# Two weight tiles of a ring of four loaded by one transfer of 1 MB instead of two of 512 KB

## The chip, the cores and the metric

One of the eight cores of a Trainium2 chip runs the kernel. Its time is the device time of one execution in microseconds (us), 738.69 us as the median of three runs. The engines are TensorE (PE, matmuls, with its weight loads as PEld), VectorE (DVE), ScalarE (ACT), GpSimd (POOL) and SyncE (SP), which here only issues DMAs. Each runs its own list of instructions in order and waits on semaphores.

## The reference

A decoder block on x of 256 tokens by 2048, all in float32. After an RMS norm one wide projection gives, for 16 heads of width 128, q, k, v and a gate, then 8 forget logits and two merge gates of 2048. Two attention branches follow, each is projected back, and the two are merged, projected and normed:

```python
z = einsum('bsd,dn->bsn', h, w_in)                   # 2048 x (8 x 1024 + 8 + 2 x 2048)
oa = diff_attention(qa, ka, va, lam)                 # 8 heads, softmax of two maps, p0 - lam * p1
ya = (rmsnorm(oa, g_subln) * (1 - lam_init) * silu(ga)) @ w_proj_a
ob = forgetting_attention(qb, kb, vb, log_f)         # 8 heads, bias by the cumulative log forget gate
yb = (ob * silu(gb)) @ w_proj_b
m = sigmoid(ma) * ya + sigmoid(mb) * yb
y = rmsnorm(x + m @ w_out, g_final)
```

## The kernel before

**Work.** The weights stream from memory, most of them through a ring (165 MB in all pass SyncE's queue, since some tiles of the gates are loaded more than once), and each is used by TensorE with the 256 tokens as stationary operand. The unit is a *tile*: 128 rows (partitions) by 1024 columns, which holds two k-steps of 128 of a chunk of 512 output columns, 512 KB. A matmul runs at high precision as three products (`split_product`, lines 342 to 344): high part of the weights times high part of the tokens, high times low, low times high. So every weight tile goes through three stations:

1. SyncE loads it into `w_raw` (four slots, `RAW = 4`), or, for one kind of tile, into `chain`.
2. ScalarE writes the high part into `w_hi` (four slots, `RING = 4`), line 614; it first waits that TensorE has used the tile four before (`w_used`).
3. VectorE writes the low part, raw minus high, into `w_lo`, line 842. This frees the slot of `w_raw` (`lo_ready`).

**Jobs.** Tiles are numbered as jobs in the order in which TensorE uses them: head 0, forget logits and part of head 1, head 2 without mixing (`PLAIN_JOB` = 20), then from `MIXED_JOB` = 28 heads 3 to 15 with 8 tiles each, mixed one to one with tiles of the merge gates, then the projection of branch B (F), of branch A (D) and the output projection (O). A head tile has two k-steps for both halves of the tokens, 12 matmuls of 512 columns. H9.2 is tile 2 of head 9. F0 is chunk 0 of the projection of branch B, which is mixed with the last gates.

**The merge gates** are computed in four groups (one for each 512 columns), each by seven products (forms P1, P5, P6, P3, P7, P4, P2) of four tiles instead of eight, in the manner of Strassen: a tile of P5, P6, P7 and P4 is a difference of a loaded tile with the one kept in `chain`. VectorE makes it with `add` (lines 855 and 857; semaphore `added`), five jobs before TensorE needs it, in its list ahead of the low split of the tile before. In forms P5, P6 and P4 the sum stands in `chain`, so the raw slot is free when the add is done. P1 tiles are loaded into `chain` itself and are not in the ring. A gate tile has 6 matmuls.

**Ring numbers.** `RAW_NO` gives each ring tile its number r; its slot is r modulo 4. `load` (in SyncE's list) waits for the user of r - 4: `added` if it is a P5, P6 or P4 tile, `lo_ready` otherwise, and issues the load. Nothing else sets the order: all lists are written out ahead of time, with no scheduler. VectorE and ScalarE also do the softmax and the gates of one head per 16 jobs, between the splits.

Of the kernel before, what the change touches and what calls it, by code (L numbers as in the profile page):

```python
# [8 lines left out]
P = 128  # L9
# [12 lines left out]
CHUNK = 512  # L22
RING = 4
RAW = 4
TILES = 8
# [4 lines left out]
P1, P5, P6, P3, P7, P4, P2 = range(FORMS)  # L30
# [5 lines left out]
MERGE, PROJ, OUT = N_HEADS, N_HEADS + 8, N_HEADS + 12  # L36

FL_JOB, VG_JOB, PLAIN_JOB, MIXED_JOB = 8, 16, 20, 28
# [3 lines left out]
OUT_JOB = DIFF_JOB + 16  # L42
# [5 lines left out]
SUM_OF = {job: s for s, job in enumerate(SUM_JOB)}  # L48
# [33 lines left out]
HEAD_OF = {head_job(c, j): (c, j) for c in range(2, N_HEADS) for j in range(TILES)}  # L82
# [4 lines left out]
def sum_parts(s):  # L87
    return s // (FORMS * QUARTERS), s // QUARTERS % FORMS, s % QUARTERS
# [7 lines left out]
JOB_OF_RAW = {r: job for job, r in RAW_NO.items()}  # L96


def add_no(s):
    g, f, q = sum_parts(s)  # L100
    return 16 * g + {P5: 0, P6: 4, P7: 8, P4: 12}[f] + q + 1


def build(nc, x, xT, xg, consts_in, w_main, w_fl, g_final, out):
    fp32 = mybir.dt.float32
    fp32r = mybir.dt.float32r
    ALU = mybir.AluOpType
# [8 lines left out]
    with ctx:  # L116
# [139 lines left out]

        def wait_raw(engine, job):
            r = RAW_NO[job]
            engine.wait_ge(raw_loaded[r % RAW], 16 * (r // RAW + 1))

        def in_chain(job):
            return job in SUM_OF and sum_parts(SUM_OF[job])[1] in (P1, P5, P6, P4)
# [9 lines left out]
        @block.sync  # L272
        def _(sp):
            def source(job):

                if job < VG_JOB:
                    return w_main[job] if job < FL_JOB else w_fl[job - FL_JOB]
                if job < PLAIN_JOB:
                    return w_main[TILES + job - VG_JOB]
                if job in HEAD_OF:  # L280
                    c, j = HEAD_OF[job]
                    return w_main[8 * c + j - 4]
                if job in SUM_OF:
                    g, f, q = sum_parts(SUM_OF[job])
                    c, half = {P1: (MERGE, 0), P5: (MERGE + 4, 0), P6: (MERGE + 4, 1), P3: (MERGE + 4, 1), P7: (MERGE, 0),
                               P4: (MERGE, 1), P2: (MERGE, 1)}[f]
                    return w_main[8 * (c + g) + 4 * half + q - 4]
                if job in FOX_OF:
                    n, j = FOX_OF[job]
                    return w_main[8 * (PROJ + n) + j]  # L290
                if job in DIFF_OF:
                    n, j = DIFF_OF[job]
                    return w_main[8 * (PROJ + n) + j - 4]
                return w_main[8 * OUT + job - OUT_JOB - 4]

            def load(job):

                if job in SUM_OF:
                    g, f, q = sum_parts(SUM_OF[job])
                    if f == P1:  # L300
                        if g == 0:
                            sp.wait_ge(sums_ready, 4)
                        else:
                            sp.wait_ge(lo_ready, SUM_JOB[SUM_OF[job] - 2 * QUARTERS] + 1)
                        sp.dma_start(chain[:, q, :], source(job)).then_inc(chain_loaded[q], 16)
                        return
                r = RAW_NO[job]
                if r >= RAW:
                    user = JOB_OF_RAW[r - RAW]
                    if in_chain(user):  # L310
                        sp.wait_ge(added, add_no(SUM_OF[user]))
                    else:
                        sp.wait_ge(lo_ready, user + 1)
                sp.dma_start(raw_slot(job), source(job)).then_inc(raw_loaded[r % RAW], 16)

            for t in range(TILES):
                if t >= 4:
                    sp.dma_start(xT_sb[:, 2 * t:2 * t + 2, :], xT[:, 2 * t:2 * t + 2, :]).then_inc(x_loaded[t], 16)
                if t == 0:
                    sp.dma_start(w_raw[:, 0, 0:CHUNK], w_main[0][:, 0:CHUNK]).then_inc(first_half, 16)  # L320
                    sp.dma_start(w_raw[:, 0, CHUNK:2 * CHUNK], w_main[0][:, CHUNK:2 * CHUNK]).then_inc(raw_loaded[0], 16)
                else:
                    load(t)
            for job in range(TILES, OUT_JOB):
                load(job)

            sp.wait_ge(o_split, 4)
            sp.dma_start(x_res, x_v).then_inc(xres_loaded, 16)
            sp.wait_ge(og_ready, N_HEADS)
            sp.dma_start(g_rows, g_final.rearrange("(a n) -> a n", a=1).to_broadcast([P, D_MODEL])).then_inc(gf_loaded, 16)  # L330
            for job in range(OUT_JOB, JOBS):
                load(job)
            for m in range(M_TILES):
                for i, cols in enumerate((DVE_OUT, LAST_OUT)):
                    sp.wait_ge(out_ready[1], 2 * m + i + 1)
                    sp.dma_start(out_v[:, m, cols], yg[:, m, cols]).then_inc(out_stored, 16)
            sp.wait_ge(out_stored, 3 * M_TILES * 16)
# [966 lines left out]
```

## Time and profile before

| | |
|---|---|
| median of 3 runs | 738.69 us (738.66 to 739.47) |
| the profiled execution's own time | 738.65 us |
| its span in the profile | 736.8 us |
| TensorE, VectorE, ScalarE busy | 99%, 76%, 60% |
| loads of w_raw of 512 KB | 283, median 4.2 us from issue to landing |

Times are from the span's start. In a timeline a row is one instruction, or several equal ones in a row (xN): its start, its duration, engine, source line, operation, what it writes and reads. Consecutive instructions of an engine overlap a little, so the start of the next is earlier than start plus duration. `[0.65 <-DMA w_raw<-in_w_main]` says that the engine was idle for 0.65 us before it and that a load's landing ended this.

### The profile page before, as it was taken

The page shows a single profiled execution, that of the slowest core. Times are in us where ns is not written, and L with a number is a line of the kernel's source. Part 1 is how long each engine was busy: PE and PEld are TensorE (multiplying, and loading weights), DVE is VectorE, ACT ScalarE, POOL GpSimd, SP SyncE. Part 2 cuts the span into 40 slices and gives each one's busy share as a digit, 9 for nine tenths or more (in the row PEclk, how much of TensorE's full clock was granted, in tenths as well). Part 3 has the DMA queues.
Part 4 walks back from the last instruction along what each step waited for, and adds up shares of the span by engine and source line. Part 5 has one row for each costly group of instructions (what it writes and reads, how often), then busy time and mean ns, then how long its engine had stood idle before and what let it go on. Part 6 is the DMA issues. An engine that isn't in the chain of part 4 may idle for free.

```text
span 736.8 us, 9631 instructions
## 1 busy us (share of the span) xinstructions
PE 727.8 (99%) x3490; PEld 606.8 (82%) x3490; DVE 560.3 (76%) x723; ACT 438.7 (60%) x652; POOL 84.7 (12%) x105
## 2 busy tenths in 40 slices
PE   9999999999999999999999999999999999999995
PEld 6998888888888888888888888888888888888884
DVE  6785799788669778868878976898998657655552
ACT  7963767566656565665666666577667544444531
POOL 0000223103010201010302020202020000001110
PEclk9999999999999999999999999999999999999999
DMA  9778366777847676775576776576777656755542
GB/s 338 210 243 296 143 229 226 233 231 254 334 151 253 210 247 231 270 293 183 212 266 202 241 274 261 191 267 222 226 246 246 207 193 230 290 190 187 194 142 115
DMA packets 47230, 168.97 MB, mean 229 GB/s; under 512 B 5256, under 2 KB 5264, under 8 KB 46672
## 3 DMA queue, kind: packets, MB, share of 16 engines
q1 hardware_dynamic: 46064, 164.97, 64.8%
q10 hardware_dynamic: 864, 1.84, 0.7%
q0 software_dynamic: 256, 1.54, 0.6%
q8 instruction: 29, 0.48, 0.3%
q14 instruction: 17, 0.14, 0.1%
HBM read 166.23 MB, written 2.11 MB: 228 GB/s over the span
## 4 chain that ended last, share of the span: by engine, by line
PE 96%; issue 1%; DMA 1%; ACT 0%; DVE 0%; SPq 0%; DVEq 0%; POOLq 0%; POOL 0%
PE Z L342 29%; PE Z L344 29%; PE Z L343 29%; PE Z L503 3%; PE A L444 1%; PE A L410 1%; DMA w_raw<-in_w_main 1%; PE B L426 1%; PE Dk L435 1%; PE B L423 1%; PE C L453 0%; PE A L461 0%; PE B L461 0%; ACT w_hi L614 0%; PE A L515 0%
## 5 line engine op out<-in xcount | busy, mean ns | idle before, releaser
L842 DVE TENSOR_TENSOR w_lo<-w_raw,w_hi 128x1024 fp32r<-128x1024 f32 (+1 forms) x240 | 290.2, 1215 | 110.7 <-ACT w_hi L614 107.9
L614 ACT ACTIVATE w_hi<-w_raw 128x1024 fp32r<-128x1024 f32 (+1 forms) x235 | 243.6, 1044 | 184.3 <-PE Z L344 149.9
L342 PE MATMUL Z<-w_hi,hT_hi 128*128 128x512 f32 (+2 forms) x720 | 275.2, 382 | 0.1
L344 PE MATMUL Z<-w_hi,hT_lo 128*128 128x512 f32 (+2 forms) x720 | 273.6, 380 | 0.0
L343 PE MATMUL Z<-w_lo,hT_hi 128*128 128x512 f32 (+2 forms) x720 | 273.5, 380 | 0.0
L342 PEld LDWEIGHTS Z<-w_hi,hT_hi 128*128 128x128 f32 x720 | 135.3, 188 | 26.6 <-ACT w_hi L614 0.5
L344 PEld LDWEIGHTS Z<-w_hi,hT_lo 128*128 128x128 f32 x720 | 135.3, 188 | 25.6
L343 PEld LDWEIGHTS Z<-w_lo,hT_hi 128*128 128x128 f32 x720 | 135.3, 188 | 25.0
L342 PE MATMUL Z<-w_hi,sum_hi 128*128 128x512 f32 x256 | 101.2, 395 | 0.0
L344 PE MATMUL Z<-w_hi,sum_lo 128*128 128x512 f32 x256 | 99.8, 390 | 0.0
L343 PE MATMUL Z<-w_lo,sum_hi 128*128 128x512 f32 x256 | 99.7, 390 | 0.0
L614 ACT ACTIVATE w_hi<-x_and_g 128x1024 fp32r<-128x1024 f32 x64 | 67.8, 1059 | 51.1 <-DVE x_and_g L857 30.2
L842 DVE TENSOR_TENSOR w_lo<-x_and_g,w_hi 128x1024 fp32r<-128x1024 f32 x64 | 80.2, 1254 | 23.2 <-ACT w_hi L614 22.2
L857 DVE TENSOR_TENSOR x_and_g<-w_raw,x_and_g 128x1024 f32<-128x1024 f32 x48 | 59.2, 1233 | 4.9 <-DMA w_raw<-in_w_main 4.9
L344 PEld LDWEIGHTS Z<-w_hi,sum_lo 128*128 128x128 f32 x256 | 48.0, 188 | 10.1
L342 PEld LDWEIGHTS Z<-w_hi,sum_hi 128*128 128x128 f32 x256 | 48.1, 188 | 9.7 <-issue 0.3
L343 PEld LDWEIGHTS Z<-w_lo,sum_hi 128*128 128x128 f32 x256 | 48.1, 188 | 9.5
L1205 POOL TENSOR_TENSOR bias<-gates,c_nat 128x128 f32<-128x128 f32 (+1 forms) x16 | 16.3, 1037 | 151.6 <-DVE neg_max L978 144.3
L1235 POOL TENSOR_TENSOR o_rstd<-o_ms,neg_half 128x2 f32<-128x2 f32 x8 | 9.2, 1156 | 190.3 <-DVE o_ms L1055 190.3
L619 ACT ACTIVATE z_sb<-Z,rstd 128x512 f32<-128x512 f32 x29 | 18.4, 685 | 20.5 <-PE Z L344 19.6
L1223 POOL TENSOR_TENSOR rope_t<-z_sb,consts 128x64 f32<-128x64 f32 x32 | 17.2, 567 | 108.4 <-ACT z_sb L619 108.4
L855 DVE TENSOR_TENSOR w_raw<-x_and_g,w_raw 128x1024 f32<-128x1024 f32 x16 | 19.7, 1229 | 5.7 <-DMA w_raw<-in_w_main 5.7
(171 smaller groups left out, 545.5 us busy)
## 6 DMA issues: line engine op xcount, KB each, us to landing
w_raw<-in_w_main SPq DMA_DIRECT2D x283, 512.0 KB, 4.2
x_and_g<-in_w_main SPq DMA_DIRECT2D x16, 512.0 KB, 6.1
w_raw<-in_w_fl SPq DMA_DIRECT2D x8, 264.0 KB, 2.9
o_T<-in_x SPq DMA_DIRECT2D x1, 2048.0 KB, 8.0
x_and_g<-in_xT SPq DMA_DIRECT2D x4, 256.0 KB, 5.8
gates<-c_rows_dram POOLq DMA_DIRECT2D x1, 1024.0 KB, 7.8
z_sb<-in_g_final SPq DMA_DIRECT2D x1, 1024.0 KB, 10.0
x_and_g<-in_xT ACTq DMA_DIRECT2D x3, 256.0 KB, 7.9
```

The costliest lines, as they stand in the source:

```text
L342: pe.matmul(acc, a_hi, b_hi, start=first, stop=False)
L343: pe.matmul(acc, a_hi, b_lo, start=False, stop=False)
L344: return pe.matmul(acc, a_lo, b_hi, start=False, stop=last)
L503: mm = pe.matmul(Z[m][:], x_part[:, 2 * j + kk, m * P:(m + 1) * P], w_part[:, kk], start=(j == 0 and part == 0 and kk == 0), stop=(j == TI ...
L614: act.activation(w_hi[:, t % RING, 0:cols_of(t)], weights(t), ACT.Copy).then_inc(hi_ready, 1)
L619: act.activation(z_sb[:, c % Z_SLOTS, m], Z[(2 if c == 2 else 0) + m][:], ACT.Copy, scale=rstd[:, m:m + 1]).then_inc(evac[m], 1)
L842: dve.tensor_tensor(w_lo[:, t % RING, 0:n], weights(t), w_hi[:, t % RING, 0:n].bitcast(fp32), ALU.subtract).then_inc(lo_ready, 1)
L855: dve.tensor_tensor(raw, chain[:, q, :], raw, ALU.subtract).then_inc(added, 1)
L857: dve.tensor_tensor(chain[:, q, :], raw, chain[:, q, :], ALU.subtract).then_inc(added, 1)
L1205: pool.tensor_tensor(bias[:, sl].unsqueeze(1), rows.rearrange("p (h n) -> p h n", h=HEADS)[:, h:h + 1, 0:n], c_nat[:, m, h:h + 1].unsqueez ...
L1223: ins = pool.tensor_tensor(rope_t[:, i], u, v, ALU.mult)
L1235: pool.tensor_tensor(o_rstd[:], o_ms[:], neg_half[:], ALU.pow).then_inc(o_rstd_ready, 1)
```

## The change

From ring number 20 on (job 20, the first tile of head 2) two consecutive ring tiles r and r + 1, r even, are loaded by one DMA into two adjacent slots (0 and 1, or 2 and 3). The weights are laid out for this ahead of time in a second array, `w_pairs`, in which each partition's row holds both tiles, 8 KB; the 16 P1 tiles and the first 20 ring tiles are still read from `w_main`. The load waits for the users of r - 4 and of r - 3, both, and is issued at the place of r. Users of both tiles wait for the one semaphore of the even slot. The lists of TensorE, ScalarE, VectorE and GpSimd keep their instructions and their order.

```diff
--- before.py
+++ after.py
@@ -96,12 +96,43 @@
 JOB_OF_RAW = {r: job for job, r in RAW_NO.items()}
 
 
+def tile_index(job):
+
+    if job < FL_JOB:
+        return job
+    if job < PLAIN_JOB:
+        return TILES + job - VG_JOB
+    if job in HEAD_OF:
+        c, j = HEAD_OF[job]
+        return 8 * c + j - 4
+    if job in SUM_OF:
+        g, f, q = sum_parts(SUM_OF[job])
+        c, half = {P1: (MERGE, 0), P5: (MERGE + 4, 0), P6: (MERGE + 4, 1), P3: (MERGE + 4, 1), P7: (MERGE, 0),
+                   P4: (MERGE, 1), P2: (MERGE, 1)}[f]
+        return 8 * (c + g) + 4 * half + q - 4
+    if job in FOX_OF:
+        n, j = FOX_OF[job]
+        return 8 * (PROJ + n) + j
+    if job in DIFF_OF:
+        n, j = DIFF_OF[job]
+        return 8 * (PROJ + n) + j - 4
+    return 8 * OUT + job - OUT_JOB - 4
+
+
+FIRST_PAIR = RAW_NO[PLAIN_JOB]
+PAIRED = len(RAW_NO) - len(RAW_NO) % 2
+
+
+def in_pair(job):
+    return FIRST_PAIR <= RAW_NO[job] < PAIRED
+
+
 def add_no(s):
     g, f, q = sum_parts(s)
     return 16 * g + {P5: 0, P6: 4, P7: 8, P4: 12}[f] + q + 1
 
 
-def build(nc, x, xT, xg, consts_in, w_main, w_fl, g_final, out):
+def build(nc, x, xT, xg, consts_in, w_main, w_pairs, w_fl, g_final, out):
     fp32 = mybir.dt.float32
     fp32r = mybir.dt.float32r
     ALU = mybir.AluOpType
@@ -256,7 +287,7 @@
 
         def wait_raw(engine, job):
             r = RAW_NO[job]
-            engine.wait_ge(raw_loaded[r % RAW], 16 * (r // RAW + 1))
+            engine.wait_ge(raw_loaded[(r - r % 2 if in_pair(job) else r) % RAW], 16 * (r // RAW + 1))
 
         def in_chain(job):
             return job in SUM_OF and sum_parts(SUM_OF[job])[1] in (P1, P5, P6, P4)
@@ -273,25 +304,7 @@
         def _(sp):
             def source(job):
 
-                if job < VG_JOB:
-                    return w_main[job] if job < FL_JOB else w_fl[job - FL_JOB]
-                if job < PLAIN_JOB:
-                    return w_main[TILES + job - VG_JOB]
-                if job in HEAD_OF:
-                    c, j = HEAD_OF[job]
-                    return w_main[8 * c + j - 4]
-                if job in SUM_OF:
-                    g, f, q = sum_parts(SUM_OF[job])
-                    c, half = {P1: (MERGE, 0), P5: (MERGE + 4, 0), P6: (MERGE + 4, 1), P3: (MERGE + 4, 1), P7: (MERGE, 0),
-                               P4: (MERGE, 1), P2: (MERGE, 1)}[f]
-                    return w_main[8 * (c + g) + 4 * half + q - 4]
-                if job in FOX_OF:
-                    n, j = FOX_OF[job]
-                    return w_main[8 * (PROJ + n) + j]
-                if job in DIFF_OF:
-                    n, j = DIFF_OF[job]
-                    return w_main[8 * (PROJ + n) + j - 4]
-                return w_main[8 * OUT + job - OUT_JOB - 4]
+                return w_fl[job - FL_JOB] if FL_JOB <= job < VG_JOB else w_main[tile_index(job)]
 
             def load(job):
 
@@ -305,12 +318,19 @@
                         sp.dma_start(chain[:, q, :], source(job)).then_inc(chain_loaded[q], 16)
                         return
                 r = RAW_NO[job]
-                if r >= RAW:
-                    user = JOB_OF_RAW[r - RAW]
-                    if in_chain(user):
-                        sp.wait_ge(added, add_no(SUM_OF[user]))
-                    else:
-                        sp.wait_ge(lo_ready, user + 1)
+                if in_pair(job) and r % 2:
+                    return
+                for slot in (r, r + 1) if in_pair(job) else (r,):
+                    if slot >= RAW:
+                        user = JOB_OF_RAW[slot - RAW]
+                        if in_chain(user):
+                            sp.wait_ge(added, add_no(SUM_OF[user]))
+                        else:
+                            sp.wait_ge(lo_ready, user + 1)
+                if in_pair(job):
+                    sp.dma_start(w_raw[:, r % RAW:r % RAW + 2, 0:2 * CHUNK],
+                                 w_pairs[(r - FIRST_PAIR) // 2]).then_inc(raw_loaded[r % RAW], 16)
+                    return
                 sp.dma_start(raw_slot(job), source(job)).then_inc(raw_loaded[r % RAW], 16)
 
             for t in range(TILES):
@@ -1289,8 +1309,10 @@
 
     xT = x[0].T.reshape(KT, P, SEQ).transpose(1, 0, 2)
     xg = np.concatenate([g_norm[0].reshape(KT, P).T, xT[:, 0:2].reshape(P, 2 * SEQ)], axis=1)
-    named = dict(x=x, xT=xT, xg=xg, consts=consts,
-                 w_main=np.concatenate(parts, axis=0), w_fl=w_fl, g_final=g_final)
+    w_main = np.concatenate(parts, axis=0)
+    in_order = [tile_index(JOB_OF_RAW[n]) for n in range(FIRST_PAIR, PAIRED)]
+    w_pairs = w_main[in_order].reshape(-1, 2, P, 2 * CHUNK).transpose(0, 2, 1, 3)
+    named = dict(x=x, xT=xT, xg=xg, consts=consts, w_main=w_main, w_pairs=w_pairs, w_fl=w_fl, g_final=g_final)
     nc = bacc.Bacc("TRN2", target_bir_lowering=False, num_devices=1)
     arrays, args = {}, []
     for name, value in named.items():
```

SyncE's list moves at two kinds of places. The first is where a new group of gates begins (group 3, during head 13), with L305/L318 the P1 loads into `chain` (named `x_and_g` there) and L314/L331 the ring loads. Before:

```order
L314 DMA w_raw<-in_w_main 128x1024 [waits lo_ready] x5
L305 DMA x_and_g<-in_w_main 128x1024 [waits lo_ready]
L314 DMA w_raw<-in_w_main 128x1024 [waits lo_ready]
L305 DMA x_and_g<-in_w_main 128x1024 [waits lo_ready]
L314 DMA w_raw<-in_w_main 128x1024 [waits lo_ready] x2
L305 DMA x_and_g<-in_w_main 128x1024 [waits lo_ready] x2
L314 DMA w_raw<-in_w_main 128x1024 [waits lo_ready] x5
```

and now:

```order
L331 DMA w_raw<-in_w_pairs 128x2048 [waits lo_ready] x3
L318 DMA x_and_g<-in_w_main 128x1024 [waits lo_ready] x2
L331 DMA w_raw<-in_w_pairs 128x2048 [waits lo_ready]
L318 DMA x_and_g<-in_w_main 128x1024 [waits lo_ready] x2
L331 DMA w_raw<-in_w_pairs 128x2048 [waits lo_ready] x2
```

Two single loads that stood on either side of a P1 load have become one pair ahead of it, and the P1 loads stand in twos behind it.

The second is SyncE's list from the middle of group 3 to the output projection, that is P3, P7, P4 and P2 of this group with head 15 and F0 and F1. Before:

```order
L314 DMA w_raw<-in_w_main 128x1024 [waits lo_ready] x17
L314 DMA w_raw<-in_w_main 128x1024 [waits added]
L314 DMA w_raw<-in_w_main 128x1024 [waits lo_ready]
L314 DMA w_raw<-in_w_main 128x1024 [waits added]
L314 DMA w_raw<-in_w_main 128x1024 [waits lo_ready] x2
L314 DMA w_raw<-in_w_main 128x1024 [waits added] x2
L314 DMA w_raw<-in_w_main 128x1024 [waits lo_ready] x28
```

and now:

```order
L331 DMA w_raw<-in_w_pairs 128x2048 [waits lo_ready] x8
L331 DMA w_raw<-in_w_pairs 128x2048 [waits added,lo_ready] x2
L331 DMA w_raw<-in_w_pairs 128x2048 [waits lo_ready]
L331 DMA w_raw<-in_w_pairs 128x2048 [waits added]
```

The run of 17 single loads has become 8 pairs that wait for two low splits each (the 17th load goes into the first pair of the next row); then two pairs wait for an add and a low split, where each load had only its own wait.

## Rows read from the trace of the kernel before

**Rows 1.** The page: busy us, share of the span, instructions.
```profile
PE 727.8 (99%) x3490; PEld 606.8 (82%) x3490; DVE 560.3 (76%) x723; ACT 438.7 (60%) x652; POOL 84.7 (12%) x105
```

**Rows 2.** Waits of TensorE: engine, line, releaser: us in total, times, longest.
```profile
PE Dk L486 <- DVE z_sb L911: 1.1, 1, 1.1
PE Z L503 <- ACT w_hi L614: 0.3, 1, 0.3
```

**Rows 3.** Waits of all engines, the same columns.
```profile
ACT w_hi L614 <- PE Z L344: 170.7, 125, 3.1
...
ACT w_hi L614 <- DMA w_raw<-in_w_main: 18.3, 18, 2.1
...
DVE w_raw L855 <- DMA w_raw<-in_w_main: 5.7, 7, 2.2
```

**Rows 4.** Windows: stretch, length, busy us (instructions) of each engine, PEclk, DMA.
```profile
520.00:555.00 35.00, 35.00 (x169) 29.09 (x168) 32.72 (x47) 23.00 (x37) 6.32 (x7) 1.00 0.71 237
...
575.00:620.00 45.00, 45.00 (x210) 37.19 (x209) 28.67 (x34) 20.72 (x28) 0.69 (x1) 1.00 0.57 188
```

**Rows 5.** Page, DMA issues: KB each, median us from issue to landing.
```profile
w_raw<-in_w_main SPq DMA_DIRECT2D x283, 512.0 KB, 4.2
...
o_T<-in_x SPq DMA_DIRECT2D x1, 2048.0 KB, 8.0
```

**Rows 6.** Loads of line 314 issued between 215.6 and 216.3 us.
```profile
L314 SPq DMA_DIRECT2D w_raw<-in_w_main x2: 327/380/432, 215.7 to 216.1; - x2
...
DMA to landing us min/median/max: 3.3/3.8/4.2
```

**Rows 7.** Loads of line 314 issued between 232 and 233.2 us.
```profile
L314 SPq DMA_DIRECT2D w_raw<-in_w_main x2: 327/380/432, 232.4 to 232.8; - x2
...
DMA to landing us min/median/max: 5.4/5.8/6.3
```

**Rows 8.** Timeline of SyncE, 519 to 522: start us, us, engine, line, operation.
```profile
519.51 0.33 SPq L314 DMA_DIRECT2D w_raw<-in_w_main  x1
...
521.25 0.33 SPq L314 DMA_DIRECT2D w_raw<-in_w_main  x1
```

**Rows 9.** Timeline of VectorE, 524 to 544; in brackets idle time before, and releaser.
```profile
524.03 1.23 DVE L855 TENSOR_TENSOR w_raw<-x_and_g,w_raw 128x1024 f32<-128x1024 f32 x1 [0.65 <-DMA w_raw<-in_w_main]
525.17 1.22 DVE L842 TENSOR_TENSOR w_lo<-w_raw,w_hi 128x1024 fp32r<-128x1024 f32 x1
...
528.62 1.22 DVE L842 TENSOR_TENSOR w_lo<-w_raw,w_hi 128x1024 fp32r<-128x1024 f32 x1
...
530.62 1.23 DVE L842 TENSOR_TENSOR w_lo<-w_raw,w_hi 128x1024 fp32r<-128x1024 f32 x1
...
532.89 1.22 DVE L857 TENSOR_TENSOR x_and_g<-w_raw,x_and_g 128x1024 f32<-128x1024 f32 x1
534.02 1.22 DVE L842 TENSOR_TENSOR w_lo<-w_raw,w_hi 128x1024 fp32r<-128x1024 f32 x1
...
543.01 1.21 DVE L857 TENSOR_TENSOR x_and_g<-w_raw,x_and_g 128x1024 f32<-128x1024 f32 x1
```

**Rows 10.** Timeline of TensorE: first matmuls of F0 and F1.
```profile
536.14 0.39 PE L342 MATMUL Z<-w_hi,sum_hi 128*128 128x512 f32 x1
...
553.25 0.39 PE L344 MATMUL Z<-w_hi,hT_lo 128*128 128x512 f32 x1
553.48 0.39 PE L342 MATMUL Z<-w_hi,sum_hi 128*128 128x512 f32 x1
```

**Rows 11.** Timeline of VectorE and TensorE at tiles H9.2 and H12.2.
```profile
295.42 1.21 DVE L842 TENSOR_TENSOR w_lo<-w_raw,w_hi 128x1024 fp32r<-128x1024 f32 x1
...
296.78 0.47 PE L342 MATMUL Z<-w_hi,hT_hi 128*128 128x512 f32 x1
...
401.40 1.22 DVE L842 TENSOR_TENSOR w_lo<-w_raw,w_hi 128x1024 fp32r<-128x1024 f32 x1
...
402.93 0.39 PE L342 MATMUL Z<-w_hi,hT_hi 128*128 128x512 f32 x1
```

## The prediction

> **What bounds the kernel now.** I read the page's busy shares first. TensorE is busy 727.8 of 736.8 us [rows 1], at a granted clock of 1.00, its upper level of 2.4 GHz, in the windows that I read [rows 4]. Then what TensorE waited for: two entries, 1.1 and 0.3 us [rows 2]. So nothing that makes a load cheaper can gain much; the question is whether a later load can reach TensorE. For that I read who waits for weight loads. ScalarE waited 18.3 us for them (18 times), VectorE 5.7 us in seven of its adds; by far the longest entry of ScalarE is TensorE, 170.7 us [rows 3]. ScalarE is thus mostly ahead and held by the four-deep w_hi/w_lo ring, but at some places a load already lands last. The windows say where this is tight: from 520 to 555 us VectorE is busy 32.7 of 35 us, from 575 to 620 only 28.7 of 45 [rows 4]. A delay of VectorE in the first can't be made up there; in the second it can.
>
> **The change, part by part.** Bytes, weights, and the work of TensorE, VectorE, ScalarE and GpSimd stay. From ring number 20 on, 272 loads of 512 KB become 136 of 1 MB.
>
> *Length of one transfer.* The trace has no 1 MB load of this form. Below: two halves issued together with nothing in flight, at 215.7 and 216.1, landed 3.3 and 4.2 us after their own issues, so both were there 4.6 us after the first [rows 6]. Further below, a single 512 KB load has a median of 4.2 us [rows 5], and I take no 1 MB load faster. Above: the 2 MB load of x with rows of 8 KB took 8.0 us [rows 5]; between 3.3 and 8.0 a line gives 4.9 for 1 MB. In trouble, two halves issued at 232.4 and 232.8 took 5.4 and 6.3, 6.7 us together [rows 7]. I take 4.7 us, near the clean rows, and keep 4.2 and 5.2 for the range.
> The Trainium skill (DMA: Bandwidth & Descriptors, Anatomy of one DMA — SWDGE (gpsimd) path) fits 2.0 us plus bytes over 436 GB/s, which is an estimate of 4.4 us here; the clean rows agree to 0.2 us. With it the walk below would give 0.7 instead of 1.6 us per stretch, and the total 744.5.
>
> *The start of a transfer.* This is the term that counts. Before, a slot was reloaded as soon as VectorE had done the low split (or the add) of its tile. Now the first slot of a pair waits for the second one's too. At 519.51 SyncE reloads slot 2, at 521.25 slot 3 [rows 8]. So the first tile of a pair loses the distance between the two releases (1.7 us here), and then the longer transfer.
>
> *Issue.* A load costs SyncE 0.33 us [rows 8]; 136 fewer save 45 us of a queue that mostly waits. Worth 0. The chain loads of form P1 now stand two behind a pair; they wait for VectorE as before and their buffer is not in the ring, so I take 0 to 0.2 us.
>
> *A walk through one stretch*, 519 to 555 us (forms P7 and P4 of the last group of merge-gate sums, with projection chunk F0 between). The starts of before are in [rows 9], TensorE's in [rows 10]; one wide VectorE operation follows another after 1.14 us, one matmul of 512 columns another after 0.23.
> - The pair of P7's third and fourth quarter: both slots free at 521.25, landed at 521.25 + 4.7 = 525.95. The add of the third quarter began at 524.03, straight on its landing. It becomes 1.9 us late.
> - VectorE is in order and without idle time from there to 535.1: split of H15.7 (525.17), softmax, add of the fourth quarter, two splits (528.62, 530.62), add of P4's first quarter (532.89), split of F0's first tile (534.02). All move 1.9 us. The last ends at 535.24 + 1.9 = 537.15. TensorE began F0 at 536.14: it stalls 1.0 us.
> - F0's second tile: its pair's slots are freed by the splits at 528.62 and 530.62, both 1.9 us late, the later at 533.75; landed 538.5, added 538.9, split done 541.0. TensorE comes to it 18 matmuls after 536.14, at 540.2, + 1.0. It just holds.
> - P4's third quarter: slots freed at 541.0, landed 545.7; its add began at 543.01, so VectorE is held again, 2.7 us, with F0's last split behind it. That ends at 548.05; TensorE comes to it 48 matmuls after 536.14, at 547.0, + 1.0. Again it just holds.
> - F1's first tile: slots free at 548.05, landed 552.8, high split 1.0, low split 1.2, done 555.1. TensorE began F1 at 553.48, + 1.0 = 554.5. Stall 0.6.
> Together 1.6 us. At 4.2 us per load it is about 0.5; at 5.2 us, since a late landing enters at three turns of the ring, 1.6 + 3 x 0.5 = 3.1.
>
> *How often.* There are four groups, each with such a stretch (near 145-190, 255-300, 390-440, 505-555). The margin before TensorE elsewhere is no larger: low splits that end at 296.63 and 402.62 are used at 296.78 and 402.93 [rows 11]; F0 had 0.9. Four times 1.6 is 6.4 us.
>
> *Spread of landings.* 4.2 us is the median, but two such transfers together took 4.6 us at one place and 6.7 at another. Before, a late load was swallowed: neither of TensorE's two entries is behind a load. Now those in the tight stretches find nothing left. Of some 34 pairs there (a quarter of 136) I let one in six land a microsecond or two late, and half a microsecond of each reach TensorE: 6 x 0.5 = 3. This is my least certain term; its ends are 0 and 8.
>
> *The rest.* From 575 on (last chunks of branch B, branch A, output projection) a tile is 12 matmuls; TensorE needs 12 x 0.23 = 2.7 us for it, 10.9 for a ring of four, against 4.7 for a landing and about 3.6 for high and low splits of a pair, and VectorE has 16 us idle in 45 [rows 4]. Worth 0. The start up to ring number 19 and the tail are untouched.
>
> Sum: 6.4 + 3 + 0.1 = 9.5 us on the profiled execution's 738.65 us (span 736.8, 1.85 us around it), which is the median of the runs (738.69) to 0.04: 748.2 us.
>
> **Rivals.**
> 1. *Absorbed.* The pair's lateness never passes the TensorE margin. For it: TensorE hardly waits now, ScalarE waits 170.7 us for TensorE, and 8 KB rows may make a landing quicker and steadier. Against it: the margins of 0.15 to 0.9 us, and a VectorE 93% busy. It decides at a lateness of 1.0 us in the P7/P4 stretches, that is a 1 MB transfer of about 3.8 us, or releases of both slots closer together. Time 738.7, up to 740. This is the case that is not slower.
> 2. *Avalanche.* One MB takes 5.2 us in the mean under load. Each turn of the ring (landing, add or high split, two low splits) is then longer than TensorE's time for four ring tiles in these stretches: 4 x 3.1 = 12.4, + 3 = 15.5, 754 us, up to 762 if the tail term grows to 8. For it: 4.9 by the x load, 6.7 in the bad row. Against it: the clean rows.
> 3. *Faster.* Half the transfers and longer rows give higher bandwidth, the waits for loads (18.3 + 5.7 us) shrink. Against it: those waits end long before TensorE's need, and the most that TensorE could get back is the 1.4 us of [rows 2]: 737.5. The Trainium skill states such a rule (DMA: Bandwidth & Descriptors, Rules for kernel authors: for bandwidth use transfers of at least 1 MiB); the trace doesn't bear it out as a gain, since a second 512 KB behind another is already there about 1.3 us after it, with its fixed part hidden.
>
> **How the numbers follow.** Forecast (2 to 14 us slower) 0.59; avalanche 0.22; absorbed 0.14; faster 0.05. A change under 0.2%, 1.5 us, can't be told from none, so: slower 0.81, same 0.14, faster 0.05. The forecast's own range is 741 to 753. The given one reaches half into the avalanche and nearly to the absorbed case: 740.5 to 758.
>
> **What would show it.** Right: 136 issues of 1 MB with a median to landing of 4.5 to 5; entries of TensorE waiting for w_lo or w_hi, 5 to 12 us together, in four clusters (150-190, 255-300, 395-440, 530-560); ScalarE's and VectorE's waits for loads up from 24 to over 100 us, ScalarE's wait for TensorE down; nothing after 575. Wrong on the start: if the 1 MB loads don't wait for the later release. Wrong on the length: a median under 4.2 or over 5.3. Wrong on the places: stalls in the output projection, or spread evenly. If TensorE shows no gaps and the time is still longer, the whole argument is wrong.

## The result, and the profile after

| | before | after |
|---|---|---|
| median of five runs each, us | 738.92 | 761.75 |
| lowest to highest, us | 738.66 to 739.49 | 759.76 to 762.67 |
| ratio, 95% interval | | 1.0303 [1.0292, 1.0315] |
| span of the profiled execution, us | 736.8 | 758.0 |

The change costs 22.8 us. The direction was forecast, the size was not: 748.2 us, with a range up to 758.

The new lines of the kernel are 20 further down where they answer to old ones (L842 is L862, L614 is L634, L342 to L344 are L362 to L364, L855 and L857 are L875 and L877). An experiment's own edit moves them by some lines more, so in its rows go by what is written and read. First the page of the kernel after: busy us, share of the span, instructions; then the chain that ended last, by engine.

```profile
PE 735.6 (97%) x3490; PEld 606.1 (80%) x3490; DVE 561.4 (74%) x723; ACT 436.4 (58%) x652; POOL 87.5 (12%) x105
...
PE 55%; DMA 19%; DVE 14%; ACT 6%; issue 4%; POOL 0%; SPq 0%; DVEq 0%; POOLq 0%; ACTq 0%
...
w_raw<-in_w_pairs SPq DMA_DIRECT2D x136, 1024.0 KB, 4.8
```

VectorE and ScalarE work as long as before [rows 1]; the time is in waits. The chain, 96% TensorE before, now runs through DMA, VectorE and ScalarE for 39%. The last line is the row of the 136 long transfers, median 4.8 us from issue to landing, where [rows 5] has 283 of 4.2.

The waits of TensorE, ScalarE and VectorE in the kernel after (us in total, times, longest), to be laid beside [rows 2, 3]:

```profile
PE Z L362 <- DVE w_lo L862: 9.1, 14, 1.9
PE Z L362 <- ACT w_hi L634: 1.8, 4, 0.7
...
ACT w_hi L634 <- DMA w_raw<-in_w_pairs: 133.6, 72, 4.8
ACT w_hi L634 <- PE Z L364: 99.9, 71, 2.9
...
DVE x_and_g L877 <- DMA w_raw<-in_w_pairs: 12.9, 12, 2.2
...
DVE w_raw L875 <- DMA w_raw<-in_w_pairs: 7.2, 7, 2.1
```

ScalarE's largest entry has changed hands: it waited 170.7 us for TensorE and 18.3 for loads, now 99.9 and 133.6. It used to be ahead and is now fed late. TensorE shows 14 waits for a low split and 4 for a high one.

How far each weight tile's last matmul lies behind the same one of before gives the delay by place. It grows in four clusters, here by the times of the kernel before: 4.1 us between 156 and 192, 4.0 between 261 and 297, 4.5 between 398 and 440, 7.3 between 509 and 556; 0.9 more at the start and 0.2 near 571. Between the clusters and after them it stays the same to 0.03 us. In all it is 21.1 us, which is the difference of the spans but for rounding.

The last cluster in the trace of the kernel after: SyncE's two loads of neighbouring pairs, and VectorE between them (start us, us; in brackets idle time and releaser).

```profile
537.93 0.33 SPq L331 DMA_DIRECT2D w_raw<-in_w_pairs  x1
...
545.14 0.33 SPq L331 DMA_DIRECT2D w_raw<-in_w_pairs  x1
```

```profile
542.70 1.22 DVE L875 TENSOR_TENSOR w_raw<-x_and_g,w_raw 128x1024 f32<-128x1024 f32 x1 [2.15 <-DMA w_raw<-in_w_pairs]
543.85 1.22 DVE L862 TENSOR_TENSOR w_lo<-w_raw,w_hi 128x1024 fp32r<-128x1024 f32 x1
...
552.54 1.34 DVE L862 TENSOR_TENSOR w_lo<-w_raw,w_hi 128x1024 fp32r<-128x1024 f32 x1
```

The pair P7.2/P7.3 (third and fourth quarter of P7) is issued at 537.93 and lands at 542.7. VectorE is idle for 2.15 us until then, before the add of P7.2 (L875). Directly behind it stands the low split of H15.7 (543.85), whose tile has lain in the *other* half of the ring since 538.15 and whose high split was done at 540.9. Only this low split frees slots 0 and 1, so their next pair (F0.0/P4.0) is issued at 545.14, not before. The two pairs, meant to be in flight side by side, go one after the other. F0.0 lands at 549.9, and its low split starts at 552.54. TensorE waits for this split:

```profile
551.74 0.40 PE L364 MATMUL Z<-w_hi,sum_lo 128*128 128x512 f32 x1
554.03 0.47 PE L362 MATMUL Z<-w_hi,sum_hi 128*128 128x512 f32 x1 [1.89 <-DVE w_lo L862]
...
555.49 0.63 PE L363 MATMUL Z<-w_lo,sum_hi 128*128 128x512 f32 x1
555.92 0.63 PE L364 MATMUL Z<-w_hi,sum_lo 128*128 128x512 f32 x1
```

The late landing of F0.0 is not what this stall is made of. VectorE has no idle time from 542.70 to 552.54, and it takes 9.84 us from the add of P7.2 to this split, where [rows 9] have 9.99 (524.03 to 534.02). What reaches TensorE is that the add of P7.2 itself is late. It starts 18.67 us later than in [rows 9], while TensorE had entered this stretch only 13.6 us later than before.

The same tie does reach TensorE one turn later, at P4.2. The chain that ended last, from 550 to 575 (start us, us, what):

```profile
550.44 4.74 DMA w_raw<-in_w_pairs
...
557.71 4.80 DMA w_raw<-in_w_pairs
...
562.54 1.23 DVE x_and_g L877
563.76 1.15 DVE w_lo L862
...
564.97 4.68 DMA w_raw<-in_w_pairs
...
572.91 0.60 DVE x_and_g L1088
...
574.21 0.47 PE Z L362
```

P4.2's pair lands at 562.5, its add runs, then the low split of F0.3 (563.76), and only now is the neighbouring pair, with F1.0, issued (564.97): two landings in a row. In this whole chain, five steps go from one pair straight to its neighbour in this way: P4.2 of group 0 (172.7 to 180.0), P7.2 of group 1 (281.8 to 289.0), P4.2 of group 2 (426.2 to 434.6), P6.2 and P4.2 of group 3 (498.0 to 505.2, 557.7 to 565.0), so one in each cluster and one ahead of the last. The other steps between weight pairs from 154 us on go to the pair that reloads the same two slots, or further.

Behind the stall of 1.89 us matmuls start 0.43 us apart instead of 0.23. The window of that stretch (busy us of each engine, PEclk, DMA share, GB/s):

```profile
554.50:557.90 3.40, 3.40 (x9) 2.65 (x9) 3.34 (x4) 2.12 (x2) 3.32 (x4) 0.50 0.89 299
```

The granted clock is 0.50 there, the lower level (1.2 GHz). Some eight intervals longer by 0.2 us cost about 1.7 us, which the 1.89 us of the stall don't contain. Of the whole difference the clock is a small part: the five executions have mean granted clocks of 0.993 to 0.996, those of the kernel before 0.996 to 0.998, which makes at most some 4 us (an estimate: 0.005 of 760 us).

### The profile page after: what moved, and what is told of

It reads as the page before. It is cut to its first block, busy times and chain, and to the rows that moved or that the text cites. A ratio compares the mean times of both kernels' runs of the same rounds, so it can differ in the third digit from the quotient of the medians.

```text
span 758.0 us, 9631 instructions
## 1 busy us (share of the span) xinstructions
PE 735.6 (97%) x3490; PEld 606.1 (80%) x3490; DVE 561.4 (74%) x723; ACT 436.4 (58%) x652; POOL 87.5 (12%) x105
## 2 busy tenths in 40 slices
DMA packets 27646, 168.96 MB, mean 223 GB/s; under 512 B 3080, under 2 KB 3088, under 8 KB 9680
## 4 chain that ended last, share of the span: by engine, by line
PE 55%; DMA 19%; DVE 14%; ACT 6%; issue 4%; POOL 0%; SPq 0%; DVEq 0%; POOLq 0%; ACTq 0%
DMA w_raw<-in_w_pairs 18%; PE Z L362 17%; PE Z L364 16%; PE Z L363 16%; DVE w_lo L862 9%; ACT w_hi L634 4%; PE Z L523 3%; DVE x_and_g L877 2%; ACT z_sb L639 1%; DVE w_raw L875 1%; DMA w_raw<-in_w_main 1%; PE A L464 1%; PE A L430 1%; PE B L446 0%; PE B L443 0%
## 5 line engine op out<-in xcount | busy, mean ns | idle before, releaser
L862 DVE TENSOR_TENSOR w_lo<-w_raw,w_hi 128x1024 fp32r<-128x1024 f32 (+1 forms) x240 | 289.8, 1215 | 125.9 <-ACT w_hi L634 123.2
L634 ACT ACTIVATE w_hi<-w_raw 128x1024 fp32r<-128x1024 f32 (+1 forms) x235 | 242.8, 1044 | 225.8 <-DMA w_raw<-in_w_pairs 133.6
L362 PE MATMUL Z<-w_hi,hT_hi 128*128 128x512 f32 (+2 forms) x720 | 277.2, 385 | 8.1 <-DVE w_lo L862 6.5
L364 PE MATMUL Z<-w_hi,hT_lo 128*128 128x512 f32 (+2 forms) x720 | 274.0, 381 | 0.0
L362 PEld LDWEIGHTS Z<-w_hi,hT_hi 128*128 128x128 f32 x720 | 135.4, 188 | 41.1 <-ACT w_hi L634 6.3
L364 PEld LDWEIGHTS Z<-w_hi,hT_lo 128*128 128x128 f32 x720 | 135.3, 188 | 26.0
L362 PE MATMUL Z<-w_hi,sum_hi 128*128 128x512 f32 x256 | 102.4, 400 | 3.9 <-DVE w_lo L862 2.6
L364 PE MATMUL Z<-w_hi,sum_lo 128*128 128x512 f32 x256 | 100.8, 394 | 0.0
L862 DVE TENSOR_TENSOR w_lo<-x_and_g,w_hi 128x1024 fp32r<-128x1024 f32 x64 | 80.9, 1266 | 20.3 <-ACT w_hi L634 19.5
L634 ACT ACTIVATE w_hi<-x_and_g 128x1024 fp32r<-128x1024 f32 x64 | 67.9, 1060 | 43.6 <-DVE x_and_g L877 27.9
L877 DVE TENSOR_TENSOR x_and_g<-w_raw,x_and_g 128x1024 f32<-128x1024 f32 x48 | 59.2, 1232 | 13.1 <-DMA w_raw<-in_w_pairs 12.9
L362 PEld LDWEIGHTS Z<-w_hi,sum_hi 128*128 128x128 f32 x256 | 48.6, 190 | 15.9 <-issue 4.4
L364 PEld LDWEIGHTS Z<-w_hi,sum_lo 128*128 128x128 f32 x256 | 48.4, 189 | 10.3
L875 DVE TENSOR_TENSOR w_raw<-x_and_g,w_raw 128x1024 f32<-128x1024 f32 x16 | 19.7, 1229 | 7.4 <-DMA w_raw<-in_w_pairs 7.2
L639 ACT ACTIVATE z_sb<-Z,rstd 128x512 f32<-128x512 f32 x29 | 18.3, 680 | 8.2 <-PE Z L364 7.3
```

The costliest lines, as they stand in the source:

```text
L362: pe.matmul(acc, a_hi, b_hi, start=first, stop=False)
L364: return pe.matmul(acc, a_lo, b_hi, start=False, stop=last)
L634: act.activation(w_hi[:, t % RING, 0:cols_of(t)], weights(t), ACT.Copy).then_inc(hi_ready, 1)
L639: act.activation(z_sb[:, c % Z_SLOTS, m], Z[(2 if c == 2 else 0) + m][:], ACT.Copy, scale=rstd[:, m:m + 1]).then_inc(evac[m], 1)
L862: dve.tensor_tensor(w_lo[:, t % RING, 0:n], weights(t), w_hi[:, t % RING, 0:n].bitcast(fp32), ALU.subtract).then_inc(lo_ready, 1)
L875: dve.tensor_tensor(raw, chain[:, q, :], raw, ALU.subtract).then_inc(added, 1)
```

## The experiments

My theory after this, here called the convoy: a pair is released by the later of two tiles and lands as one, and in the four clusters VectorE's order ties one pair's release to the other pair's landing, so that two landings stand in one turn of the ring (a turn is the reload of all four slots). The rivals: the *length* (or form) of a 1 MB transfer; the *start* alone (the joint release, my prediction's main term); the joint *landing* alone.

**1. Joint release alone.** The pair's load waits for both slots, then goes as two transfers of 512 KB, each with its own semaphore:

```
-   sp.dma_start(w_raw[:, r % RAW:r % RAW + 2, ...], w_pairs[...]).then_inc(raw_loaded[r % RAW], 16)
+   for one in (r, r + 1):
+       sp.dma_start(raw_slot(JOB_OF_RAW[one]), source(JOB_OF_RAW[one])).then_inc(raw_loaded[one % RAW], 16)
```

> Only the joint release stays: the load of a pair still waits for both slots, but goes as two 512 KB transfers back to back, each with its own landing. Length (the 1 MB transfer itself is what costs): the first tile of a pair lands about 4.2 us after its issue again, the second 0.33 us later plus a little, so most of the 22.8 us goes: 739 to 743. Start (my prediction's term, the wait for the later of two releases): this stays whole, and it was to be the larger part: 750 to 760. Convoy (the joint release and the joint landing couple: two tiles are freed late because both landed late): either half alone does little, 739 to 743, with TensorE's entries of waiting for low splits under 3 us against 9.1. Length and convoy read alike here; the other kernels part them.

Measured: 742.84 us, ratio 1.0046 [1.0032, 1.0060], so +3.9 us. Length and convoy had 739 to 743, the start alone 750 to 760: the term on which I had built the forecast is worth little by itself.

**2. Joint landing alone.** Every slot has its own 512 KB load and its own release, as before; who uses a tile waits for both loads of the pair:

```
-   engine.wait_ge(raw_loaded[(r - r % 2 if in_pair(job) else r) % RAW], 16 * (r // RAW + 1))
+   for one in (r - r % 2, r - r % 2 + 1) if in_pair(job) else (r,):
+       engine.wait_ge(raw_loaded[one % RAW], 16 * (r // RAW + 1))
```

> Only the joint landing stays: each slot is reloaded by its own 512 KB transfer as soon as it alone is free, as in the kernel before, but whoever uses a tile of a pair waits for both tiles of the pair. Start: the joint release is gone, so 739 to 741. Length: 739 to 741, too, since there is no 1 MB transfer. If the joint landing alone were the cost (the first tile of a pair is held by the second, which was freed 1.7 us later): 755 or more. Convoy: 740 to 742.

Measured: 746.70 us, 1.0103 [1.0088, 1.0118], +7.8. More than the convoy's 740 to 742, less than the 755 of "landing alone". ScalarE's wait for loads is 104.6 us in its trace. I had underrated this half; it is not the whole either.

**3. Rows of 4 KB.** The same 136 transfers and waits, the weights laid out so that a transfer has two rows of 4 KB per partition instead of one of 8.

> The changed kernel with the same 136 transfers of 1 MB, the same waits, and rows of 4 KB instead of 8 KB (256 rows per transfer, two per partition). Form of the transfer (8 KB packets of 309 ns against 4 KB packets of 159): if the long rows are what makes it slow, the median to landing falls under 4.6 us and the time to about 745. Start and convoy: the waits are the same, so 760 to 765, unless the landing's median moves from 4.8 us; every 0.3 us of it is worth about 6 us.

Measured: 761.91 us, 1.0312 [1.0295, 1.0329]; median to landing 4.8 us again. The form of the rows makes no difference, although the number of the whole kernel's packets goes from 27,646 to 45,054.

**4. The add behind the split.** The kernel after, with VectorE's order changed where a gate tile opens a pair:

```
+   opens_pair = adds and RAW_NO[job + 5] % 2 == 0
+   if adds and not opens_pair:
        add(SUM_OF[job + 5])
    split(job + RING)
+   if opens_pair:
+       add(SUM_OF[job + 5])
```

> The changed kernel with one order changed: where a gate tile opens a pair, VectorE does the low split of the tile five jobs before first and the add of the gate tile behind it. In the changed kernel this add stands in front of the split, and waits for its pair to land, while the split is what frees the slots of the other pair. Convoy: the two pairs' loads then no longer wait for each other; the four clusters of TensorE's delay shrink from 21 us together to 7 to 11, and the time falls to 746 to 752. Start alone or length alone: the releases stay joint and the transfers stay 1 MB, so within 2 us of 761.75, or longer, as the add comes later.

Measured: 752.22 us (748.12 to 753.32), 1.0162 [1.0140, 1.0184], +13.3. No transfer, byte or release rule differs from the kernel after, and 9.5 of 22.8 us are gone. The edit moves only 9 of the 64 adds, since in `RAW_NO` only these open a pair. In the trace the chain no longer goes from a pair straight to its neighbour (that execution, 748.12 us, is the shortest of the five). So the gain is by the convoy's mechanism, but the time is 0.2 us outside the 746 to 752 that it expected, and more than half of the loss stays.

**5. Both joints, short transfers.** Edits 1 and 2 together: joint release, two 512 KB transfers, users wait for both.

> Both joints and no long transfer: a pair's load waits for both slots, goes as two 512 KB transfers back to back, and whoever uses a tile waits for both landings. Joint release alone cost 3.9 us and joint landing alone 7.8. Convoy (the two couple): more than their sum, 14 to 20 us, so 753 to 759, with four clusters of delay as in the changed kernel; what is missing to 22.8 is then the length, the landing of the second half at about 4.5 us against 4.8. Length: if the 1 MB transfer itself carries the rest, the two add up and no more: 12 us, 749 to 752. If 8 KB or 1 MB mattered for nothing and landings alike: 762.

Measured: 761.90 us, 1.0312 [1.0287, 1.0337], +22.9: the whole loss, without one 1 MB transfer, and more than the 753 to 759 of the convoy; it is the 762 of "mattered for nothing". Its rows, DMA issues and waits:

```profile
w_raw<-in_w_main SPq DMA_DIRECT2D x283, 512.0 KB, 4.2
...
PE Z L363 <- DVE w_lo L863: 8.6, 12, 1.9
...
ACT w_hi L635 <- DMA w_raw<-in_w_main: 143.6, 74, 5.9
ACT w_hi L635 <- PE Z L365: 91.5, 65, 2.7
```

The median of a load is 4.2 us as in [rows 5], the waits are much like those of the kernel after. So it makes no difference whether a pair is one transfer or two. That two halves and one whole of 1 MB are about equally late shows too: from the first issue of a pair to both landed took 4.65 us in the median here (mean 5.13), the 1 MB transfers 4.81 (mean 5.05). Both are longer than the 4.2 us of one half; that part of the length belongs to the joint landing. And the halves don't add: 3.9 + 7.8 = 11.7; the other 11.2 us exist only when both are there.

**6. Pairs only outside the clusters.** in_pair() is false for four stretches of ring numbers, those of forms P7 and P4 with some P3 and P2 beside them. The expectation says more than the edit does: gate tiles of P5 and P6, which also stand among head tiles, keep their pairs, and so do four of the nine adds that open one. (The trace has 84 transfers of 1 MB, not the 88 that I wrote.)

> Pairs only where no gate tile stands among the head tiles: ring numbers 56 to 81, 102 to 123, 160 to 183 and 206 to 237 keep single loads of 512 KB as in the kernel before; 88 of 136 transfers of 1 MB stay. Place (convoy in the four stretches with merge-gate sums): nothing is lost, 738.5 to 740. Length (a 1 MB load costs wherever it stands): 65% of 22.8 us stays, 753.

Measured: 741.54 us, 1.0027 [1.0017, 1.0037], +2.5. The place rules, not the number of transfers: 62% of the pairs cost 11% of the loss. But it is more than the 738.5 to 740 that I had expected. Its loads:

```profile
w_raw<-in_w_pairs SPq DMA_DIRECT2D x84, 1024.0 KB, 4.8
w_raw<-in_w_main SPq DMA_DIRECT2D x115, 512.0 KB, 4.4
```

**7. Pairs only in the last cluster** (ring numbers 206 to 237).

> Pairs only in the last of the four stretches (ring numbers 206 to 237, 16 transfers of 1 MB), the one that my prediction walked. Its walk gave 1.6 us, and 3 us of spread over four stretches, so 2 to 3 us: 741 to 742. In the changed kernel this stretch lost 7.3 us. If it does so by itself: 745 to 748. If its loss needs what earlier stretches left (a later start of the ring): near 741.

Measured: 747.99 us, 1.0127 [1.0105, 1.0148], +9.0 from 16 transfers. This is the stretch to which my walk had given 1.6 us. It doesn't need what earlier stretches left.

**8. Pairs that open at odd ring numbers.** The same transfers, 135 of them, the ring's slots shifted by one; each pair now joins the second tile of an old pair with the first of the next.

> The same 1 MB transfers with pairs that open at odd ring numbers (135 of them; the slots of the ring are shifted by one so that a pair stays side by side in memory). Each pair then opens with the second tile of a former pair, so that every add of a gate tile at an odd place in VectorE's order now waits for the pair behind it, and the low split that it stands in front of frees that pair's partner. Number and length of transfers are the same. Length: about 762. Start alone (distance between two releases, on average the same): 755 to 770. Convoy: it depends on how VectorE's adds stand to the pairs, and here more of them stand wrong: well over 790, up to 860.

Measured: 872.23 us, 1.1803 [1.1774, 1.1831], +133 us, beyond even the 860 that the convoy was given. Of the 64 adds 55 now open a pair, where it was 9. The adds wait:

```profile
PE 771.2 (89%) x3490; PEld 621.3 (71%) x3490; DVE 559.8 (64%) x723; ACT 434.0 (50%) x652; POOL 78.5 (9%) x105
...
PE Z L374 <- ACT w_hi L646: 61.1, 33, 3.9
...
DVE x_and_g L889 <- DMA w_raw<-in_w_pairs: 112.1, 38, 4.4
DVE w_raw L887 <- DMA w_raw<-in_w_pairs: 35.5, 13, 4.6
```

VectorE's adds waited 147.6 us for loads (20.1 in the kernel after), with transfers of the same size and the same 4.8 us. Beside the waits TensorE is busy 35.6 us longer than in the kernel after; its mean granted clock over the span is 0.963. The tie by itself, from the chain that ended last:

```profile
162.69 4.81 DMA w_raw<-in_w_pairs
...
167.53 1.23 DVE w_raw L887
168.75 1.15 DVE w_lo L874
...
169.96 4.69 DMA w_raw<-in_w_pairs
```

A landing, an add, a low split, and the next pair is issued: 7.3 us for a pair (a head tile and a gate tile, 18 matmuls) for which TensorE needs 18 x 0.23 = 4.1.

**9. VectorE's new order in the kernel before.** Edit 4 with single loads.

> The kernel before (single loads) with the edit of VectorE's order alone: the same adds of gate tiles go behind the low split. Convoy: this order costs only because of the pairs, so the edit is worth nothing here: 738.5 to 739.5. If the adds' place were bad or good for itself, so that the 9.5 us that it gave back in the changed kernel have nothing to do with pairs: faster or slower by more than 2 us.

Measured: 738.89 us, 0.9999 [0.9990, 1.0007]. The order is worth nothing without pairs.

**10. Exactly the pairs of the walk** (ring numbers 218 to 237).

> Pairs only for ring numbers 218 to 237, from the third and fourth quarter of P7 in the last group on: exactly the ten pairs of my prediction's walk, and every tile before them comes as in the kernel before, so that the walk is entered with no lateness. My walk gave 1.6 us, plus at most 1 of spread: 740.3 to 741.6. With pairs from ring number 206 on it was 9.0. If the walk was right and only its entry wrong: within 1 us of 740.5. If the walk itself left something out (the landing at 4.95 instead of 4.7 between a freed slot and its use, the split of H15.7 behind an add that waits): 742 to 744.

Measured: 744.57 us, 1.0080 [1.0065, 1.0095], +5.6, against 1.6, and above both of the ranges expected. The trace of its profiled execution (748.16, the longest of six) shows the walk as it really goes. VectorE:

```profile
527.00 1.22 DVE L877 TENSOR_TENSOR w_raw<-x_and_g,w_raw 128x1024 f32<-128x1024 f32 x1 [3.28 <-DMA w_raw<-in_w_pairs]
528.15 1.22 DVE L864 TENSOR_TENSOR w_lo<-w_raw,w_hi 128x1024 fp32r<-128x1024 f32 x1
...
536.84 1.34 DVE L864 TENSOR_TENSOR w_lo<-w_raw,w_hi 128x1024 fp32r<-128x1024 f32 x1
...
548.59 1.23 DVE L879 TENSOR_TENSOR x_and_g<-w_raw,x_and_g 128x1024 f32<-128x1024 f32 x1 [3.12 <-DMA w_raw<-in_w_pairs]
549.73 1.22 DVE L864 TENSOR_TENSOR w_lo<-w_raw,w_hi 128x1024 fp32r<-128x1024 f32 x1
...
556.94 1.23 DVE L864 TENSOR_TENSOR w_lo<-w_raw,w_hi 128x1024 fp32r<-128x1024 f32 x1 [2.44 <-ACT w_hi L636]
...
558.94 1.27 DVE L1090 SCALAR_TENSOR_TENSOR x_and_g<-gates,Z 128x512 f32<-128x512 f32 x2
```

TensorE:

```profile
538.33 0.47 PE L364 MATMUL Z<-w_hi,sum_hi 128*128 128x512 f32 x1 [1.68 <-DVE w_lo L864]
...
560.31 0.77 PE L364 MATMUL Z<-w_hi,sum_hi 128*128 128x512 f32 x1 [3.49 <-DVE x_and_g L1090]
```

The add of P7.2 is 2.97 us later than in [rows 9], not 1.9: the low split that frees the pair's second slot ended at 522.15 in this execution, and the pair was issued at 522.24, not 521.25; it landed after 4.7 us, as assumed. The next pair, F0.0/P4.0, landed at 534.1, well before its turn on VectorE. F0.0's split is late by 2.8, and TensorE stalls 1.68 us where the walk has 1.0. Then P4.2's pair takes 6.5 us to land, 1.8 more than in the walk. The add that waits for it (548.59) stands ahead of F0.3's split (549.73), which frees slots 0 and 1. So the next pair, with F1.0, is issued at 551.02 and lands at 555.8. F1.0's low split waits for that (556.94), and behind it in VectorE's order stands the projection gate product (L1090), for which TensorE waits 3.49 us, as it frees banks of Z. The walk had F1's weights at 555.1 and a stall of 0.6; here they are there at 558.2, and the gate product is done 2 us later still. That last wait is not one for a weight at all. In experiment 7, where the same pair landed after 4.8 us, the same line still held TensorE for 3.0 us: there too two transfers stood in a row.

**11 and 12. The new order with each half.** Edit 4 on experiment 1, and on experiment 2.

> Two 512 KB loads behind a joint release (742.8 in the run before), and VectorE's low split in front of the adds that open a pair. What is left of the joint release alone if the order no longer ties two pairs together: convoy 739 to 741; start alone, as the distance between two releases is the same: 742 to 744.

> Each slot reloaded by its own 512 KB transfer as soon as it is free, users wait for both landings of a pair (746.7 in the run before), and VectorE's low split in front of the adds that open a pair. With this the eight combinations of joint release, joint landing and VectorE's order are all but complete. Convoy: an add that waits for a pair held the split that frees the other pair's slot, so this falls to 740 to 743. If the joint landing costs for itself, whatever the order on VectorE: 745 to 748. If the gain of the new order needs the joint release, too: 746 to 747.

Measured: 739.63 us, 1.0010 [1.0001, 1.0018], +0.7; and 745.17 us, 1.0065 [1.0048, 1.0081], +5.85 against its runs of before. The first is within the convoy's 739 to 741. The second is what "the joint landing costs for itself" expected, not the convoy's 740 to 743. What the joint release costs is nearly all the tie on VectorE; what the joint landing costs is mostly its own.

All together, us over the kernel before:

| | old order on VectorE | add behind the split |
|---|---|---|
| single loads | 0 | -0.05 |
| joint release | 3.9 | 0.7 |
| joint landing | 7.8 | 5.85 |
| both, two of 512 KB | 22.9 | not run |
| both, one of 1 MB | 22.8 | 13.3 |

No version beats the kernel before. The best with 1 MB transfers is experiment 6, 2.5 us behind it.

## Why the prediction was wrong

**What held.** That it gets slower, and by what kind of wait. All of the four places, and nothing after 575 (the last 0.2 us come near 571). 136 issues with a median of 4.8 us (4.5 to 5 forecast, 4.7 used). TensorE's entries for w_lo and w_hi at L362 are 10.9 us in total (5 to 12), ScalarE's and VectorE's waits for loads 153.7 us (over 100). ScalarE waits less for TensorE. That larger transfers bring nothing here held also. Experiments 3 and 5 are the evidence: neither the rows nor the size of a transfer moved the time by more than the intervals tell. The rule of the Trainium skill (DMA: Bandwidth & Descriptors, Rules for kernel authors), at least 1 MiB per transfer for bandwidth, shows no gain in any run here. The Trainium skill (DMA: Bandwidth & Descriptors, Anatomy of one DMA — SWDGE (gpsimd) path) would have 4.4 us for 1 MB, an estimate from its fit for transfers issued by GpSimd; the trace has 4.8 for these, issued by SyncE.

**The step that failed: "Together 1.6 us", and with it "Four times 1.6 is 6.4 us".** Experiment 10 measures the walk by itself at 5.6 us, experiment 7 the whole stretch at 9.0. In the kernel after the four stretches lost 4.1, 4.0, 4.5 and 7.3 us in the profiled execution, 19.9 where walk and spread had 9.4. Three things were wrong in it:

1. *The tie between the pairs.* The walk follows it once: P4.2's add waits, F0.3's split stands behind it and frees F1's pair. That is the tie which the chain shows too. But the walk stops at F1's weights and leaves out the gate product behind their split, for which TensorE waited 3.49 us in experiment 10 and 3.0 in experiment 7, where the walk has 0.6. (At H15.7 the same order stands and the walk doesn't follow it. This did no harm: the tied pair landed at 534.1 in experiment 10 and 549.9 in the kernel after, its split had its turn on VectorE at 536.84 and 552.54.) Experiment 4 shows all ties together at 9.5 us (22.8 to 13.3), experiments 1 and 11 at 3.2 of 3.9.
2. *The joint landing.* In the walk the second tile of a pair gains what the first loses, and I priced the first only where its own use was tight. Experiment 2 has 7.8 us, 5.85 of them without the tie. And release and landing don't just add: 11.2 us appear only with both. Why so much of this stays with the new order (13.3 against 0.7 + 5.85, so 6.7 us) the runs don't take apart; this part of the cause stays open.
3. *The entry.* The walk began at 519.5 with nothing late and at 521.25 with its first issue. The stretch in the kernel after begins earlier, among the P3 tiles, and the turn is already behind when it comes to P7. From 508 us (in times of before) to F0.0's first matmul TensorE falls back by 4.3 us in the kernel after, by 4.0 in experiment 7, whose pairs begin at P3, and by 1.8 in experiment 10, whose pairs begin with the walk; the walk has 1.0. By the medians experiment 7 has 3.4 us more than experiment 10. This may also be why a late landing costs more than the half microsecond per turn that I gave it: the ring hadn't made up what it had lost before the next late one came. That was not tested.

**The sentence "This is the term that counts", on the start of a transfer,** fell with experiment 1: 3.9 us, of which 0.7 are left once VectorE's order is changed. The start counts in company.

**The spread of landings** (3 us, ends 0 and 8) was set as a term beside the walk, at half a microsecond for each late pair. At the tie a late landing is passed on whole to the next pair, as at 548.59 in experiment 10 (6.5 us, VectorE idle 3.12). What the spread costs is not measured apart from the rest.

**Not priced at all:** the bank that a late gate product holds (L1090: 3.49 us in experiment 10, 0.9 in the kernel after), and the clock: 1.7 us in one stretch of the kernel after.

**The rivals.** The avalanche (754 to 762) had the time nearest to the result and its mechanism in part: a turn of the ring longer than TensorE's time (in the chain of the kernel after 12.5 us from 537.93 to 550.44, for P7.2, P7.3, F0.0 and P4.0, 30 matmuls or 6.9 us). Its condition, a mean of 5.2 us for 1 MB, wasn't quite met (5.05) and wasn't needed, since experiment 5 does the same with loads of 4.2. It should have had more than 0.22, for a reason that stood in part in the order of VectorE's list and not in any duration.

## What to carry to other kernels

When two buffers are joined in one transfer, draw for each pair who frees its last slot, and what stands ahead of that instruction on its engine. If it is something that waits for the *other* pair, the transfers no longer overlap, and the ring's turn holds two landings. The order of an engine's list then sets a part of the cost that no transfer's length shows: here 9.5 of 22.8 us from nine adds, and with 55 adds in such a place the loss grew to 133 us. In a walk through a profile, follow every moved instruction to what it releases and to what stands behind it on its engine, and start the walk where the change starts, not where the stretch looks tight. And two joints that cost little each (here 3.9 and 7.8 us) may cost twice their sum when they stand together.

## What the runs showed of the hardware

- Rows of 4 and of 8 KB make the same landing: medians of 4.77 and 4.81 us for 1 MB (experiment 3 and the kernel after). Two 512 KB transfers issued one behind the other are both there after 4.65 (experiment 5).
- The granted clock doesn't follow from one stall's length. A stall of 1.89 us in the kernel after was followed by the window at 0.50 above. In experiment 7 a stall of the same 1.89 us, before the same tile F0.0, and one of 3.0 us before F1 left it at 1.00 (its upper level, 2.4 GHz):

```profile
540.37 0.47 PE L364 MATMUL Z<-w_hi,sum_hi 128*128 128x512 f32 x1 [1.89 <-DVE w_lo L864]
```

```profile
540.40:544.00 3.60, 3.60 (x16) 2.97 (x17) 3.46 (x3) 1.94 (x2) 3.52 (x4) 1.00 0.86 309
561.00:567.00 6.00, 6.00 (x35) 5.02 (x36) 4.22 (x5) 1.12 (x2) 0.00 (x0) 1.00 0.62 203
```

  In the profiled execution of experiment 10 the granted clock is 0.50 from 559.2 to 566.0, and thirteen matmuls ran at this lower level after the stall of 3.49 us, about 2.6 us more. Its other five executions are 3 to 4 us shorter; that the clock is the reason was not shown.
